# High and low halves of the activations interleaved word by word in a float32r hybrid trunk

## The reference, cut to what matters

```python
h = h + stick_breaking_mixer(rmsnorm(h, sb_norm[j]), sb_w_qkv[j], sb_w_o[j])
h = h + swiglu_ffn(rmsnorm(h, ffn_norm[i]), ffn_w_gate_up[i], ffn_w_down[i])
# mixer 0: h @ w_qkv (2048 x 6144), o @ w_o (2048 x 2048)
# mixer 1: gelu(h @ w_in) (2048 x 4096), (u * mixed) @ w_o (2048 x 2048)
# swiglu:  (silu(gate) * up) @ w_down, gate_up 2048 x 11264, w_down 5632 x 2048
```

## Time and profile before

| | us |
|---|---|
| median of 2 executions | 2097.78 |
| lowest, highest | 2097.65, 2097.91 |
| span of the profiled execution | 2097.8 |

### The profile page before, as it was taken

How to read it: one execution, slowest core, us unless ns; L and a number is a source line. 1 busy time by engine, 2 the same in 40 slices (tenths; PEclk the granted TensorE clock), 3 DMA queues, 4 the chain that set the end, 5 groups by cost and what they waited for, 6 DMA issues and landing times.

```text
span 2097.8 us, 27159 instructions
## 1 busy us (share of the span) xinstructions
PE 2088.2 (100%) x9281; PEld 1729.4 (82%) x9281; DVE 1430.7 (68%) x1822; ACT 1013.1 (48%) x1285; POOL 16.4 (1%) x30
## 2 busy tenths in 40 slices
PE   9999999999999999999999999999999999999998
PEld 7888888888888888888888888888888888888887
DVE  6787777867666676665557887877666676664444
ACT  6577765544444444444445444554444444444443
POOL 1000000000000000000000000000000000000000
PEclk9999999999999999999999999999999999999999
DMA  8555554666666666555566665566666666655554
GB/s 264 179 179 170 181 189 167 198 196 192 191 190 198 191 193 195 192 191 196 194 192 209 190 200 183 190 190 201 192 189 198 192 193 194 190 194 198 192 191 150
DMA packets 207419, 402.47 MB, mean 192 GB/s; under 512 B 12336, under 2 KB 13056, under 8 KB 206976
## 3 DMA queue, kind: packets, MB, share of 16 engines
q1 hardware_dynamic: 206496, 398.11, 61.1%
q0 software_dynamic: 688, 3.18, 0.4%
q10 hardware_dynamic: 176, 0.40, 0.1%
HBM read 399.55 MB, written 2.10 MB: 191 GB/s over the span
## 4 chain that ended last, share of the span: by engine, by line
PE 99%; issue 0%; DMA 0%; DVE 0%; ACT 0%; POOLq 0%; POOL 0%; DVEq 0%; SPq 0%
PE acc L1085 64%; PE acc L1091 32%; PE tp L1156 0%; PE tp L1176 0%; PE acc L1106 0%; PE acc L1107 0%; PE acc L1108 0%; PE tp L1302 0%; DMA h<-in_x 0%; PE tp L1116 0%; PE acc L1345 0%; PE acc L1344 0%; PE acc L1343 0%; PE acc L1143 0%; PE tp L1136 0%
## 5 line engine op out<-in xcount | busy, mean ns | idle before, releaser
L654 DVE TENSOR_TENSOR w_lo<-raw,w_hi 128x1024 fp32r<-128x1024 f32 x750 | 916.0, 1224 | 584.9 <-ACT w_hi L348 581.1
L348 ACT ACTIVATE w_hi<-raw 128x1024 fp32r<-128x1024 f32 x750 | 792.9, 1060 | 922.4 <-PE acc L1091 917.2
L1085 PE MATMUL acc<-w_hi,xT 128*128 128x512 f32 x4032 | 998.7, 390 | 0.0
L1085 PEld LDWEIGHTS acc<-w_hi,xT 128*128 128x128 f32 x4032 | 756.0, 188 | 155.9
L1091 PE MATMUL acc<-w_lo,xT 128*128 128x512 f32 x2016 | 539.2, 389 | 0.0
L1091 PEld LDWEIGHTS acc<-w_lo,xT 128*128 128x128 f32 x2016 | 378.6, 188 | 78.5
L1085 PE MATMUL acc<-w_hi,hid_hi 128*128 128x512 f32 x944 | 368.7, 391 | 0.0
L1085 PE MATMUL acc<-w_hi,hid_lo 128*128 128x512 f32 x944 | 367.6, 389 | 0.0
L1091 PE MATMUL acc<-w_lo,hid_hi 128*128 128x512 f32 x944 | 252.5, 389 | 0.0
L1091 PEld LDWEIGHTS acc<-w_lo,hid_hi 128*128 128x128 f32 x944 | 177.3, 188 | 36.7
L1085 PEld LDWEIGHTS acc<-w_hi,hid_hi 128*128 128x128 f32 x944 | 177.3, 188 | 36.8
(11 more groups left out here) (115 smaller groups left out, 477.6 us busy)
## 6 DMA issues: line engine op xcount, KB each, us to landing
raw<-in_ffn_w_gate_up SPq DMA_DIRECT2D x352, 512.0 KB, 4.5
raw<-in_ffn_w_down SPq DMA_DIRECT2D x176, 512.0 KB, 3.6
raw<-in_sb_w_qkv SPq DMA_DIRECT2D x95, 512.0 KB, 4.3
raw<-in_gm_w_in SPq DMA_DIRECT2D x64, 512.0 KB, 4.4
raw<-in_sb_w_o SPq DMA_DIRECT2D x32, 512.0 KB, 4.1
raw<-in_gm_w_o SPq DMA_DIRECT2D x32, 512.0 KB, 4.0
h<-in_x SPq DMA_DIRECT2D x3, 512.0 KB, 7.6
gain_bc<-in_gm_v_norm POOLq DMA_DIRECT2D x1, 1024.0 KB, 6.1
```

The source lines that it names most:

```text
L348: nc.scalar.activation(w_hi[:, p % RING], raw[:, p % RING], ACT.Copy).then_inc(hi_ready, 1)
L654: nc.vector.tensor_tensor(w_lo[:, p % RING], raw[:, p % RING], w_hi[:, p % RING].bitcast(f32), ALU.subtract).then_inc(lo_ready, 1)
L1085: nc.tensor.matmul(acc_at(chunk, r), part[:, kt, rs], w_hi[:, p % RING, k], start=(kt == 0 and part is hi), stop=False)
```

## The change

The two halves are interleaved word by word. In `xT`, the dimension of size 2 (high, low) becomes the innermost one. In the region, `hid_hi` and `hid_lo` become the two interleaved halves of one tensor `hid`. Each written, read back or loaded run of 128, 256 or 1,024 words now has a step of 8 bytes instead of 4. The sizes are the same, and instructions, their number, their order and their waits too. The offsets of what is laid over the region follow: `FREE` goes from 16,384 to 32,768 bytes, since the 16 interleaved tiles that these stages use now stand together, and `MORE` is 61,440 bytes, which is what `HB + FREE` was.

```diff
-        xT = sb("xT", [P, KD, 2, S], f32r)
-        xT_hi, xT_lo = xT[:, :, 0], xT[:, :, 1]
+        xT = sb("xT", [P, KD, S, 2], f32r)
+        xT_hi, xT_lo = xT[:, :, :, 0], xT[:, :, :, 1]
...
-        HB = KF * S * 4
...
-        hid_hi = at("hid_hi", 0, [P, KF, S], f32r)
-        hid_lo = at("hid_lo", HB, [P, KF, S], f32r)
+        hid = at("hid", 0, [P, KF, S, 2], f32r)
+        hid_hi, hid_lo = hid[:, :, :, 0], hid[:, :, :, 1]
         rows_first = at("rows_first", 0, [KD, P])
-        FREE = KD * S * 4
+        FREE = 2 * KD * S * 4
+        MORE = FREE + (KF - KD) * S * 4
...
-        prob_blk = at("prob_blk", HB + FREE + 5 * CB, [P, ZW])
+        prob_blk = at("prob_blk", MORE + 5 * CB, [P, ZW])
...
-        q_t = at("q_t", HB + FREE, [P, HG, S])
-        k_t = at("k_t", HB + FREE + CB, [P, HG, S])
-        vn = at("vn", HB + FREE, [P, RT, D])
-        wsT = at("wsT", HB + FREE + RT * D * 4, [P, KD, P])
+        q_t = at("q_t", MORE, [P, HG, S])
+        k_t = at("k_t", MORE + CB, [P, HG, S])
+        vn = at("vn", MORE, [P, RT, D])
+        wsT = at("wsT", MORE + RT * D * 4, [P, KD, P])
```

## The result

| | before | changed |
|---|---|---|
| median, us | 2097.78 | 2157.24 |
| span of the profiled execution, us | 2097.8 | 2155.5 |
| ratio, 95% interval | | 1.0284 (1.0254 to 1.0314) |

What follows compares the result with a forecast made beforehand. The prediction took TensorE's matmul steps as the bound and added 0 us each for loads, writers and moved arrays to 2097.8 us, giving 2097.8 us. The range was 2092 to 2125 us.

Steps and rivals of the forecast that it cites:

- What bounds the kernel: Whole kernel: TensorE bounds it, 9,024 matmul steps of 226.7 ns making 2045.8 us, 97.5% of the span.
- The load itself: Stationary tile loads on TensorE: 113 ns with the 8-byte step against 106 today, all hidden, so 0 us.
- The writers: VectorE and ScalarE writing the tiles: taken as 0 us; if each word doubled in price, at most +3.4 us.
- What it moves: Arrays over the region go up 16,384 bytes with the same contiguous pattern; no DMA, wait or queue changes, 0 us.
- rival 1: TensorE's steps: load disturbs the moving stream, the 13.4 ns excess doubles, +121 us, 2218.7 us; chance 0.10.
- The argument against rival 1: TensorE's steps: `xT` and hidden tiles lie elsewhere against the weights, yet both take 226.7 ns; nothing ties excess to load.
- The span "is the median too": Starting figure of the sum: the profiled span of 2097.8 us equals the median, so no offset was added.

Runs made afterwards that it cites:

- xT_only: Kernel before with only `xT` interleaved word by word, the region left as it was; 2137.86 us.
- pair_8: Kernel before with words of feature tiles 2n and 2n+1 alternating in `xT` (step 8 bytes), high and low parts lying apart; 2157.18 us.
- n384_alternate: Changed kernel with matmuls streaming 384 of 512 columns, save in the first product, the last pieces and each chunk's first matmul; 1724.12 us.
- one_column: Kernel before with each load reading one column 128 times, save in pieces of the first product and the last ones; 2128.64 us.
- apart_x128_r64: Kernel before, contiguous tiles, with `xT` 128 and the region 64 bytes further along against the weights; 2151.51 us.

## Why the prediction was wrong, point by point

- **What bounds the kernel**: right. TensorE's step times 9,024 is 98% of the time, before and after, and the whole loss lies in it.
- **The load itself**: right. The estimate was 113 ns in place of 106; the next load starts after 0.11 in place of 0.10 us, the record grows by 5 ns, and nothing waits for it. What doubles it is a step of 16 bytes.
- **The writers**: 0 taken, upper bound a doubling. VectorE 0, ScalarE 1,026 to 1,101 ns, all hidden. Right; the slowing by 1.7 to 2 times comes at 16 bytes.
- **What it moves**: right (`xT_only`: the region's steps are what they were when only `xT` is changed, and `pair_8`, which keeps the old offsets, is as slow).
- **The step that failed** is the one from "the load is hidden" to "0 us". A load that nobody waits for was given the price nothing; its price is what it does to the step of the matmul beside it, +6.7 ns, and so the sum's 0 measured +59.5 us. That was rival 1, with a chance of 0.10 and a price of 13.4 ns (2218.7 us). Its mechanism is right in that the loss comes by way of the load and is paid in the step, and its size was twice too large, because it let a fixed excess of 13.4 ns grow with the stretch that is walked; `n384_alternate`, with twice the stretch and the same excess of 13.3 ns, and `one_column` show that it does not behave so. The loss lay above the 4.7 ns that it named as the deciding point, and the range stopped at 3 ns.
- **The argument against rival 1 did not hold.** It said that `xT` and hidden tiles stand at different places against the weights and have like steps. The places differ, but only by multiples of 512 bytes, by construction. The code says so, in `lead_in` and in the assertion on `R0`, and that line should have raised the question of what happens elsewhere. `apart_x128_r64` answers it: 232.2 and 233.3 ns.
- **The span "is the median too"**: a coincidence. The profiled execution of the kernel before was 1.7 us slower than the median: its first matmul steps took 0.43 us, those of the changed kernel 0.23 (8.00, 8.22, 8.46 us), and its steady run began 1.3 us later (at 28.8 in place of 27.5 us). That is why the spans differ by 57.7 us and the medians by 59.5. It has no part in the loss.

What stays open is the mechanism under it. Shown: the loss is in TensorE's step and comes by way of the tile that is loaded; it depends on that tile's address and on the step between its columns; at 512 columns it lies between 0 and 6.7 ns with contiguous tiles and between 3.3 and 6.7 with alternate ones, at the places tried; with fewer columns it falls, in the alternate layout at 0 bytes to 3.3 ns at 448 and 0 at 384, with contiguous tiles at their bad places to 2.5 and 1.4 ns at 384. That two read streams meet in the same part of the memory fits the dependence on address and step, and for that there is only this argument; why the loss falls so fast with columns that stream after the load has ended, no run tells. All shifts moved the loaded tiles and none the weights, so whether the place relative to the weights counts or the tile's own address, modulo 512 bytes, isn't separated. Nor was `w_lo` shifted against `w_hi`, a place finer than 32 bytes tried, or a matmul run without a load beside it, which would tell whether the 13.3 ns belong to the load.

## What to carry to other kernels

Where TensorE is the bound and each matmul has its own load, take the step from the starts in the timeline and compare it with the columns at the granted clock; a few ns over thousands of matmuls are per cents, and no wait, idle time or busy share shows them. The place of the stationary tiles, modulo 512 bytes, is worth up to 6.7 ns of 227 here, with the same instructions (0 and 256 bytes gave the same step in both layouts, and 192 and 448 in the one where both were run). So alignment code in a tuned kernel is a hint to try what happens elsewhere, and a new layout needs its own search over places before it is judged (here 2157 us falls to 2130 and not to 2098). A step of 8 bytes in these operands costs the load or writer itself 0 to 7%; at 16 bytes a load and the large writers take 1.7 to 2 times as long.

## What the runs showed of the hardware that was not expected

- A hidden load of a stationary tile lengthens the step of the matmul beside it by 0 to 6.7 ns according to the tile's address. The load's own record stays at 188 ns while contiguous tiles lose 6.7, and is 5 to 8 ns longer with alternate ones.
- The loss of the alternate layout at 0 bytes is 6.7, 3.3 and 0 ns at 512, 448 and 384 streamed columns.
- At the good places (contiguous, 0 and 256 bytes) a float32r step has 13.3 ns over its columns at 512 (226.7), and so it has at 384 (173.3, both layouts at 0 bytes).
- A load of one column repeated 128 times is worse for its neighbour (up to 231.2 ns) than a load of 128 different ones at the same place (226.7).
- At a step of 16 bytes the next load begins 0.21 us after one that starts alone, which is less than the old matmul step, and yet the step becomes 235.0 ns; at 32 bytes it is 244 ns. Writers of 1,024 words go from 1,026 to 2,051 ns (ScalarE, 16 bytes) and from 1,218 to 2,287 ns (VectorE, 32 bytes).
